# Moving operand tiles 1152 bytes apart in a TensorE kernel for a hybrid decoder step

## The reference

```python
h = h + 0.5 * gt1[:, None] * swiglu(modulate(h, p['norm_ffn1'][l], sh1, sc1),
                                    p['w_ffn1_up'][l], p['w_ffn1_down'][l])
y, nh, ns, nkv = mixer(modulate(h, p['norm_mix'][l], shm, scm), pos, conv_hist, s0, kv_bufs, p, l)
h = h + gtm[:, None] * y
h = h + 0.5 * gt2[:, None] * swiglu(modulate(h, p['norm_ffn2'][l], sh2, sc2),
                                    p['w_ffn2_up'][l], p['w_ffn2_down'][l])
...
return rmsnorm(h, p['norm_final']), new_states
```

## Time and profile before

| | |
|---|---|
| median of 3 runs | 2664.78 us (2663.97 to 2665.51) |
| profiled execution, from its first to its last instruction (span) | 2663.4 us |
| PE busy with matmuls | 2614.3 us (98%) |
| DVE busy | 1415.9 us (53%) |
| ACT busy | 1053.7 us (40%) |
| granted TensorE clock, mean | 0.996 |

### The profile page before, as it was taken

The page is one execution under the profiler, slowest core; times in us unless marked ns, Lnnn a source line. Parts: engine busy times, 40 slices in busy tenths (PEclk is TensorE's granted clock), DMA queues, the critical chain, the costliest instruction groups (busy, mean ns, idle before and its releaser), DMA issues.

```text
span 2663.4 us, 49403 instructions
## 1 busy us (share of the span) xinstructions
PE 2614.3 (98%) x21449; PEld 2466.8 (93%) x21449; DVE 1415.9 (53%) x1803; ACT 1053.7 (40%) x1086; POOL 24.1 (1%) x49
## 2 busy tenths in 40 slices
PE   7999999999999999999999999999999999999998
PEld 4889999999999889999989999899999999999997
DVE  3554455444455766655566554375644455444455
ACT  4343333333344423744434444343433333333443
POOL 0000000000000000000000000000000000000000
PEclk9999999999999999999999999999999999999999
DMA  9987755777666687433267565778456655555453
GB/s 398 386 300 279 254 189 185 250 252 266 243 232 214 227 316 285 150 125 127 103 226 266 218 234 214 278 280 308 174 206 237 220 176 193 186 189 174 159 184 130
DMA packets 127376, 601.39 MB, mean 226 GB/s; under 512 B 10336, under 2 KB 10592, under 8 KB 81136
## 3 DMA queue, kind: packets, MB, share of 16 engines
q1 hardware_dynamic: 121360, 573.68, 60.1%
q0 software_dynamic: 5280, 24.79, 2.5%
q10 hardware_dynamic: 576, 0.56, 0.1%
HBM read 586.36 MB, written 12.62 MB: 225 GB/s over the span
## 4 chain that ended last, share of the span: by engine, by line
PE 93%; DVE 3%; DMA 2%; ACT 1%; issue 1%; DVEq 0%; SPq 0%; ACTq 0%; POOLq 0%
PE acc L2131 48%; PE acc L2141 24%; PE acc L2432 5%; PE mp L2220 4%; PE acc L2437 2%; PE acc L2317 2%; PE mp L2116 1%; PE acc L2342 1%; DMA raw<-in_ada 1%; PE mp L2498 1%; PE mp L2503 1%; DVE wlo L1372 1%; PE mp L2198 1%; ACT whi L895 1%; DMA h<-in_x 0%
## 5 line engine op out<-in xcount | busy, mean ns | idle before, releaser
L1372 DVE TENSOR_TENSOR wlo<-raw,whi 128x2048 fp32r<-128x2048 f32 (+2 forms) x427 | 888.8, 2082 | 706.5 <-ACT whi L895 703.9
L895 ACT ACTIVATE whi<-raw 128x2048 fp32r<-128x2048 f32 (+2 forms) x427 | 743.8, 1742 | 478.2 <-PE acc L2141 388.7
L2131 PEld LDWEIGHTS acc<-xhi,whi 128*128 128x128 f32 x3808 | 476.1, 189 | 44.9 <-issue 43.9
L2131 PE MATMUL acc<-xhi,whi 128*128 128x264 f32 x3808 | 508.1, 286 | 3.6 <-ACT whi L895 3.0
L2131 PE MATMUL acc<-xlo,whi 128*128 128x264 f32 x3808 | 499.4, 284 | 0.0
L2141 PE MATMUL acc<-xhi,wlo 128*128 128x264 f32 x3808 | 498.6, 284 | 0.0
L2131 PEld LDWEIGHTS acc<-xlo,whi 128*128 128x128 f32 x3808 | 476.6, 188 | 0.0
L2141 PEld LDWEIGHTS acc<-xhi,wlo 128*128 128x128 f32 x3808 | 475.7, 188 | 0.0
L2141 PE MATMUL acc<-uhi,wlo 128*128 128x264 f32 x1408 | 191.6, 284 | 0.0
L2131 PE MATMUL acc<-uhi,whi 128*128 128x264 f32 x1408 | 190.7, 283 | 0.0
L2131 PE MATMUL acc<-ulo,whi 128*128 128x264 f32 x1408 | 190.1, 283 | 0.0
(11 more groups left out here) (391 smaller groups left out, 1958.9 us busy)
## 6 DMA issues: line engine op xcount, KB each, us to landing
raw<-in_up SPq DMA_DIRECT2D x160, 1024.0 KB, 4.8
raw<-in_ada SPq DMA_DIRECT2D x136, 1024.0 KB, 8.0
raw<-in_down SPq DMA_DIRECT2D x128, 704.0 KB, 4.1
raw<-in_win SPq DMA_DIRECT2D x69, 1024.0 KB, 5.0
raw<-in_wgate SPq DMA_DIRECT2D x32, 1024.0 KB, 4.8
blk<-in_up SPq DMA_DIRECT2D x16, 1024.0 KB, 7.9
raw<-in_wout SPq DMA_DIRECT2D x16, 1024.0 KB, 5.5
raw<-in_wproj SPq DMA_DIRECT2D x24, 512.0 KB, 4.9
```

Of the source, the lines that this page charges most:

```text
L895: act.activation(whi[:, s.slot(SPLIT), 0:width], raw[:, r.slot(RAW), 0:width], ACT.Copy)\
L1372: v.tensor_tensor(wlo[:, s.slot(SPLIT), 0:width], raw[:, r.slot(RAW), 0:width], whi[:, s.slot(SPLIT), 0:width].bitcast(F32), ALU.subtract)\
L2131: mm(dst, whi[:, b, (tile + k) * P:(tile + k + 1) * P], x[part], start=starts and part == 0 and k == 0, stop=False)
```

## The change

The tiles of `xhi`, `xlo`, `uhi` and `ulo` get a pitch of `TP` = 288 columns, 1152 bytes (4 times 256 and 128), of which 264 columns are used. `xhi` begins 64 bytes later. With the start bytes that the build gives, the tiles of `xhi`, `xlo` and `uhi` then have places 64, 192, 64, 192, ..., and those of `ulo` 192, 64, 192, .... `wlo` and `whi` stay where they are. No matmul is added, removed or moved.

To find the room, small things move: four of the nine parts of `mod` go into the unused 24 columns behind the `x` tiles (strided by 1152 bytes now); the two `blk` buffers and the partial sums lie in the tail of `uhi` and `ulo`; `park_lo` becomes two halves, one of them over `sg` and `hf`; the first `stash` lies in the `x` tiles as pieces of 256 columns, so each of its loads becomes two DMAs; `vs` moves down by 448 bytes, over the end of a buffer whose contents are stored by DMA, so ACT waits for that store before it first writes `vs`.

```diff
+TP = 288
...
         h = place("h", [KD, NT])
-        xhi_at = cursor[0]
-        xhi = place("xhi", [KD, NT], F32R)
-        xlo = place("xlo", [KD, NT], F32R)
...
-        mod = place("mod", [NADA, MW])
+        xhi_at = cursor[0] + 64
+        assert whi_at % 128 == 0 and xhi_at % 128 == 64
+        x_tiles = [place("xhi", [KD, TP], F32R, xhi_at), place("xlo", [KD, TP], F32R)]
+        xhi, xlo = (x[:, :, 0:NT] for x in x_tiles)
+        x_spare = [place(f"x_spare{b}", [KD, TP], F32, xhi_at + 4 * KD * TP * b) for b in range(2)]
+        mods = [place(f"mod{m}", [KD, MW]) for m in range(NMOD - 4)]
+        mods += [x[:, :, c:c + MW] for x in x_spare for c in (NT, NT + MW)]
...
-        uhi = place("uhi", [HALF, NT], F32R, body)
-        ulo = place("ulo", [HALF, NT], F32R)
...
+        ulo_at = body + 4 * HALF * TP + 128
+        u_end = ulo_at + 4 * (HALF * TP - (TP - NT))
+        assert body % 128 == 64
+        uhi = place("uhi", [HALF, TP], F32R, body)[:, :, 0:NT]
+        ulo = place("ulo", [HALF, TP], F32R, ulo_at)[:, :, 0:NT]
...
-        vs = place("vs", [G, NT], F32, late)
+        vs = place("vs", [G, NT], F32, late - 448)
...
+                for b in range(AG // T):
+                    at = AG * m + T * b
+                    pool.dma_start(stash[n][m][:, ATL * b:ATL * (b + 1), :],
+                                   t["ada"][first:first + 13:4, :, at:at + T].rearrange("c p x -> p c x"))\
+                        .then_inc(stash_loaded, 16)
...
-                if sl and g == 0:
-                    act.wait_ge(v_stored, 16 * sl)
-                    act.wait_ge(v_turned, 2 * sl)
+                if g == 0:
+                    if sl:
+                        act.wait_ge(v_stored, 16 * sl)
+                        act.wait_ge(v_turned, 2 * sl)
+                    else:
+                        wait_stored(act, 2)
...
-                v.tensor_tensor(park_lo[:, :], raw[:, r.slot(RAW), :], park_hi[:, :].bitcast(F32), ALU.subtract)\
-                 .then_inc(slot_done[r.slot(RAW)], 1)
+                for b, low in enumerate(park_lo):
+                    w = slice(PANEL // 2 * b, PANEL // 2 * (b + 1))
+                    last = v.tensor_tensor(low[:, :], raw[:, r.slot(RAW), w], park_hi[:, w].bitcast(F32), ALU.subtract)
+                last.then_inc(slot_done[r.slot(RAW)], 1)
```

More of the change, by code:

```diff
@@ L341, in build @@
         raw = place("raw", [RAW, PANEL])
+        whi_at = cursor[0]
         whi = place("whi", [SPLIT, PANEL], F32R)
         wlo = place("wlo", [SPLIT, PANEL], F32R)
+        h_at = cursor[0]
         h = place("h", [KD, NT])
-        xhi_at = cursor[0]
-        xhi = place("xhi", [KD, NT], F32R)
-        xlo = place("xlo", [KD, NT], F32R)
[L348 to L351, removed]
-        mod = place("mod", [NADA, MW])
+        xhi_at = cursor[0] + 64
[5 more added lines that the diff above has]
+        mods += [x[:, :, c:c + MW] for x in x_spare for c in (NT, NT + MW)]
         par = place("par", [PAR_W])
@@ L370, in build @@
         body = cursor[0]
-        uhi = place("uhi", [HALF, NT], F32R, body)
-        ulo = place("ulo", [HALF, NT], F32R)
[L374 to L377, removed]
+        ulo_at = body + 4 * HALF * TP + 128
[3 more added lines that the diff above has]
+        ulo = place("ulo", [HALF, TP], F32R, ulo_at)[:, :, 0:NT]
+        blk, parts = [], []
+        for name, first, end in (("g", body, ulo_at), ("u", ulo_at, u_end)):
+            blk.append(place(f"blk_{name}", [PANEL], F32, end - 4 * PANEL, end))
+            part_at = end - 4 * PANEL - 4 * NBLK // 2 * NT
+            assert part_at >= first + 4 * (NBLK // 2 - 1) * TP
+            parts.append(place(f"part_{name}", [NBLK // 2, NT], F32, part_at, end))
+        part_g, part_u = parts
+        sg_at = u_end
+        sg = place("sg", [2, NT], F32, sg_at)
         hf = place("hf", [2, NT])
+        sq_at = cursor[0]
         sq = place("sq", [2, NT])
@@ L508, in build, with mod @@
         sacco = place("sacco", [NT])
-        stash.append([place(f"stash1{m}", [PANEL], F32, oT_at + 4 * m * PANEL, gt_at + 4 * KD * NT) for m in range(4)])
+        stash = [[x_spare[m // 2][:, KD // 2 * (m % 2):KD // 2 * (m % 2 + 1), 0:T] for m in range(4)],
+                 [place(f"stash1{m}", [PANEL // T, T], F32, oT_at + 4 * m * PANEL, gt_at + 4 * KD * NT)
+                  for m in range(4)]]
+        def mod(q, n):
+            m, k = divmod(q, KD)
+            return mods[m][:, k:k + n, :]
         def gates(q, n=1):
@@ L969, in norm @@
                     act.activation(xhi[:, k, 0:T], t1[:, k % 2, :], ACT.Identity,
-                                   bias=mod[:, shift + k, 0:1]).then_inc(x_hi, 1)
+                                   bias=mod(shift + k, 1)[:, 0, 0:1]).then_inc(x_hi, 1)
             def tiles(base, i, stride):
@@ L1059, in start_hi @@
                     act.wait_ge(panel_used, s - 1)
-                act.activation(whi[:, s % 2, :], blk[:, s % 2, :], ACT.Copy).then_inc(hi_done, 1)
+                act.activation(whi[:, s % 2, :], blk[s % 2][:, :], ACT.Copy).then_inc(hi_done, 1)
             def block_taken(b):
@@ L1484, in norm @@
                     dve.wait_ge(x_hi, q0 + k + 2)
-                    v.scalar_tensor_tensor(xlo[:, k, 0:T], t1[:, k % 2, :], mod[:, shift + k, 0:1],
+                    v.scalar_tensor_tensor(xlo[:, k, 0:T], t1[:, k % 2, :], mod(shift + k, 1)[:, 0, 0:1],
                                            xhi[:, k, 0:T].bitcast(F32), ALU.add, ALU.subtract)\
```

42 lines of the change are left out of this document (19 added, 23 removed).

## The result

The changed kernel takes 2603.19 us (median of 4 runs, 2600.95 to 2604.01) against 2664.66 us before: a ratio of 0.9767, 95% interval 0.9753 to 0.9781, or 61.5 us less. The profiled execution is the fastest of the four, so its span fell by a little more, 64.8 us. The forecast was 2634 us, 31 us less: the direction was right and the time lies in the range, but the gain is twice the one forecast.

A forecast was written before the change was run, and what follows sets the result against it. The prediction took PE's matmuls to bound the kernel: 2663.4 − 31 (matmul step) + 0.3 (`park_low`) = 2632.7 us of span; with the runs' median 1.4 us above it, 2634 us, range 2580 to 2690.

The forecast's parts named there:

- the middle of the two bounds: Step assumed for the large matmuls after the new pitch: 119 ns, −1.8 × 17,184 = −31 us; called a choice, not a measurement.
- the lower bound: Shortest step of a large matmul in the earlier trace, 116 ns against 120.8; worth −82 us over 17,184 matmuls.
- The upper bound: Slowest step with the moving operand at one place, 122.5 ns; +29 us over the large matmuls.
- the fixed runs: Rows of the earlier trace, eight matmuls each, with the moving operand at one place: 121.2, 122.5 and 120 ns a step.
- What bounds the kernel: Whole kernel: PE, busy 2614.3 of 2663.4 us; 17,184 large matmuls at 120.8 ns, so 1 ns of step is worth 17.2 us.
- That the place matters: Large passes: some 4% of a step goes with the tile's place; single durations by tile pair ran from 280 to 288 ns.
- Rival B: Large matmuls: places only shift the step between neighbours, mean stays 120.8 ns; 2665 us, chance 0.11.
- The 112.5 ns: Estimate for a 264-column matmul from the skill's N / 2.4 GHz plus about 2.5 ns; by that alone near 2522 us.
- Rival C: Large matmuls: alternating places 64 and 192 cost 121.6 ns a step, +14 us, 2679 us; chance 0.30.
- Rival D: PE gets faster and becomes the engine that waits, for DVE or ACT; given no chance of its own.
- The side edits: `park_low` in halves at two seams costs 0.3 us; doubled `stash` loads and ACT's wait before `vs` cost 0 each.
- The first stage: First 133 us: DMA engines 99% busy, transfers set the end, so its matmuls gain nothing and were not counted.

## Why the prediction was wrong

**The step that failed is the size of one term**: "I take the middle of the two bounds, 119 ns". The step is 116.7, 0.7 above the lower bound of 116 that the shortest duration gave, so the term is −70 us and not −31. The upper bound and the pull towards it came from the earlier trace rows: "the fixed runs stand nearer to the upper end". These rows have the place of afterwards and yet don't price it, because in them the place is repeated. The first block shows it directly: 121.2 ns in the changed kernel too, while its panels run at 116.7; and taking the even tiles first brings 122.5 into a panel. The prediction doubted these rows, but for another reason (each run is only eight long and begins from a jump), and let them set the bound and the mean. The lower bound, worked out from the shortest duration, was right to a nanosecond.

**That the direction came out right was in part luck.** Nothing in the prediction says why 64 and 192 should be good places. By the earlier trace rows the pairs that begin at 0 and 128, with 284 and 280 ns, look better than those that begin at 64 and 192, with 283 and 288, so the same argument would have forecast a gain for tiles at 0 and 128, and that kernel is 17 us slower than the one before. The 64 bytes decide, and the prediction had no price for them.

**What bounds the kernel** held: PE, at 98% before and after, and 17.2 us a nanosecond. With 116.7 ns the prediction's own sum gives 2663.4 − 70.5 + 0.3 = 2593.2 us of span, 5.4 below the 2598.6 measured, about what the waits added.

**That the place matters** held, with a correction: I spoke of the tile's place and of a drift against weight blocks at place 0. Moving only the weights gives the same 2681 us as moving only the tiles, so it is the distance. Rival B (places only shift the step between neighbours) fell with it. The Trainium skill, "TensorE: Matmul & The Clock Gate", section "Step-by-step: what each phase is for", has it that loading the next weights takes no read bandwidth from the running matmul, by its two read ports; here 64 bytes in the address of the weights alone change the step of the matmul by 5 ns (116.7 to 121.7), so in these runs load and matmul are not independent. That it is the two reads that collide is the nearest reading of the runs, not something that a row shows. The 112.5 ns that the prediction takes from the Trainium skill, "TensorE: Matmul & The Clock Gate", section "Back-to-back issue gap", is there the gap of a single matmul by itself, not of a stream in which each has a load; no pass of 264 columns in these runs is faster than some 116.7 ns a step.

**Rival C** (slower, 2679 us) lies within 2 us of the changed kernel without its 64 bytes, 2681. That is a coincidence: C was worked out for the places 64 and 192.

**Rival D** had no chance of its own, and the 5.6 us lost to waits, nearly all for `w_ada` and for DVE at the seams, are this rival in small: they were missing from the sum.

**The side edits** stayed within their prices. DVE's two halves of `park_low` take 2.36 us together for 2.29, and PE's wait behind them is the same 2.10 us as in the earlier trace rows:

```profile
858.99 2.36 DVE L1471 TENSOR_TENSOR park_lo<-raw,park_hi 128x1024 fp32r<-128x1024 f32 x2 [0.49 <-ACT park_hi L975]
```

PE waits for ACT's `whi` for 3.5 us in all, 3.9 before, and nowhere for `stash`, so no row shows a cost of ACT's new wait or of the doubled loads. Behind the waits at the first seam (PE worked for 3.36 of the 5.40 us up to 870.40) the granted clock is 0.51, the level of 1.2 GHz, from 871.5 to 874.9, and matmuls start 0.22 us apart. The kernel before has such a stretch in its first stage (0.52 from 156.0 to 159.5, behind a wait of 1.77 us for `w_ada`), about as long, so the comparison of the two profiles loses little by it.

**The first stage**, left out of the sum because transfers set its end, did not stay as it was. The pass with `wlo` of its third last block begins at the same time before and after (150.13 and 150.11), but the first panel behind the stage begins 3.1 us earlier:

```profile
172.08 2.21 PE L2131 MATMUL acc<-xhi,whi 128*128 128x264 f32 x16 [0.53 <-DVE part_g L1613]
```

```profile
168.94 2.17 PE L2153 MATMUL acc<-xhi,whi 128*128 128x264 f32 x16 [0.53 <-DVE part_g L1635]
```

Some 1.6 us of this the kernel before lost by its stretch of low clock (16 matmuls in 3.57 us where 1.95 is usual there). Up to 133 us the DMA engines are 100% busy in the changed kernel, with PE at 111.0 us.

## What to carry to other kernels

These runs price float32r matmuls of 264 columns, in one kernel. Where matmuls with a load of their own for each are the bound, look at single durations by tile before believing that a shape has one price: a spread of 3% over equal shapes is a reason to try other layouts, and here the shortest of them was the better guide to what a good layout gives than short runs at the same address. It tells how much there is to gain and not at which addresses. Set the bytes between the weights and the moving tiles, and the change of place from one matmul to the next, together, across the seams of passes too. Try moving one operand alone by 64 bytes: the program's work stays the same, and here it was worth 78 us.

## What the runs showed of the hardware

- Distances of 64 modulo 128 between weight block and tile, with the tile's place alternating by 128 modulo 256, give 116.7 ns for 264 columns; 0, 32, 96, 48 and 80, or a repeated place, 119 to 123 (48 and 80 with half loads). In a cycle that drifts by 32 bytes the rule does not hold: there the pair at 128 and 160 is the short one.
- The state has a memory: a pass at the good distance behind a colliding one took 1.88 to 1.91 us for its 16 matmuls in place of 1.86, and one of 11 matmuls had a mean of 283 in place of 278. A pass behind a `w_ada` panel begins slowly as well.
- A whole weight load of 128 float32r columns sets the step of short matmuls: 192 and 128 columns both take 1.23 to 1.24 us for a pass of 11, and 192 take 1.02 with half a load.
- Open: why 116.7 ns and not less for 264 columns, which half a load doesn't change; why 256 columns are no faster; why place 128 is fast in the drifting cycle; why weights read from column 16 did not help behind slow passes; and why a repeated place collides where an alternating one does not.
